# A four-layer transformer kernel on one core: products of a block of ones in TensorE's waits at twelve layer norms and two RMS norms

## What is computed

```
def layer_norm(x, g, b):
    mu = jnp.mean(xf, axis=-1, keepdims=True)
    var = jnp.mean(jnp.square(xf - mu), axis=-1, keepdims=True)
    y = (xf - mu) * lax.rsqrt(var + LN_EPS) * g + b
...
    for i in range(DEPTH_2):
        y = swa_sink_attention / rglru_block / mla_attention (x, ...)
        x = layer_norm(ALPHA * x + y, ln_g[i, 0], ln_b[i, 0])
        x = layer_norm(ALPHA * x + memory_cross_attention(x, ...), ln_g[i, 1], ln_b[i, 1])
        x = layer_norm(ALPHA * x + conv_glu_ffn(x, ...), ln_g[i, 2], ln_b[i, 2])
```

## Time and profile before

| | us |
|---|---|
| median of three runs | 2805.81 |
| lowest and highest run | 2800.55 and 2807.04 |
| span of the profiled execution, first to last instruction | 2794.0 |
| median less span | 11.8 |
| TensorE matmuls busy | 2636.5 |
| TensorE weight loads busy (beside matmuls) | 2501.8 |
| GpSimd busy | 1819.7 |
| ScalarE busy | 1467.7 |
| VectorE busy | 1126.3 |
| mean granted TensorE clock, share of full | 0.963 |

### The profile page before, as it was taken

One profiled execution on the slowest core, in us unless ns is written; L12 is line 12 of the kernel. 1 busy time (PEld: TensorE's weight loads), 2 busy tenths in 40 slices (PEclk: granted clock), 3 DMA queues, 4 the chain that ended last, 5 costly groups with the idle time before them and its releaser, 6 DMA issues.

```text
span 2794.0 us, 52649 instructions
## 1 busy us (share of the span) xinstructions
PE 2636.5 (94%) x19840; PEld 2501.8 (90%) x19840; DVE 1126.3 (40%) x2642; ACT 1467.7 (53%) x2586; POOL 1819.7 (65%) x770
## 2 busy tenths in 40 slices
PE   7998889999999999989999998999999999989998
PEld 5897779999997799988899988899978999988998
DVE  5227634122155521135443365433443433553334
ACT  5336734445445554444555576555645555555655
POOL 0446647878875778863578865488645688535886
PEclk7999999999999999999999999999999999989998
DMA  6324424555553555542345543355423455323554
GB/s 228 125 102 153 146 95 166 180 178 184 183 167 126 180 168 183 179 142 81 121 151 181 185 138 128 107 189 180 157 92 121 144 181 183 127 76 121 173 180 136
DMA packets 115637, 421.75 MB, mean 151 GB/s; under 512 B 12832, under 2 KB 14112, under 8 KB 114976
## 3 DMA queue, kind: packets, MB, share of 16 engines
q1 hardware_dynamic: 115200, 417.00, 45.2%
q10 hardware_dynamic: 288, 2.62, 0.2%
HBM read 418.52 MB, written 1.05 MB: 150 GB/s over the span
## 4 chain that ended last, share of the span: by engine, by line
PE 58%; issue 18%; POOL 15%; DVE 5%; ACT 2%; DMA 1%; POOLq 0%; SPq 0%; DVEq 0%; ACTq 0%
POOL ring_low L2444 15%; PE bank L610 10%; PE bank L611 10%; PE bank L616 10%; PE bank L601 7%; PE bank L602 7%; PE bank L603 7%; PE bank L916 2%; PE bank L885 2%; PE bank L766 1%; DMA ring<-in_units 1%; PE bank L705 1%; PE bank L934 1%; PE bank L706 1%; PE bank L899 1%
## 5 line engine op out<-in xcount | busy, mean ns | idle before, releaser
L2444 POOL TENSOR_TENSOR ring_low<-ring,ring_high 128x1024 fp32r<-128x1024 f32 x766 | 1819.5, 2405 | 954.5 <-ACT ring_high L1243 744.0
L610 PE MATMUL bank<-high,ring_high 128*128 128x256 f32 (+1 forms) x3372 | 857.1, 290 | 3.2 <-ACT ring_high L1243 1.8
L611 PE MATMUL bank<-low,ring_high 128*128 128x256 f32 (+1 forms) x3372 | 849.5, 288 | 0.0
L610 PEld LDWEIGHTS bank<-high,ring_high 128*128 128x128 f32 x3372 | 647.0, 192 | 10.5 <-ACT ring_high L1243 3.5
L611 PEld LDWEIGHTS bank<-low,ring_high 128*128 128x128 f32 x3372 | 647.2, 192 | 6.5
L1475 ACT ACTIVATE ring_high<-ring 128x1024 fp32r<-128x1024 f32 x448 | 468.3, 1054 | 90.8 <-DMA ring<-in_units 90.8
L616 PE MATMUL bank<-high,ring_low 128*128 128x256 f32 (+1 forms) x3372 | 491.3, 288 | 0.3 <-POOL ring_low L2444 0.3
L616 PEld LDWEIGHTS bank<-high,ring_low 128*128 128x128 f32 x3372 | 444.9, 192 | 6.1 <-POOL ring_low L2444 0.5
L1243 ACT ACTIVATE ring_high<-ring 128x1024 fp32r<-128x1024 f32 x337 | 351.4, 1054 | 101.1 <-DMA ring<-in_units 99.7
L601 PE MATMUL bank<-hid_high,ring_high 128*128 128x256 f32 x1232 | 349.5, 284 | 9.8 <-DVE hid_low L2091 7.4
L602 PE MATMUL bank<-hid_low,ring_high 128*128 128x256 f32 x1232 | 348.6, 283 | 0.0
(11 more groups left out here) (226 smaller groups left out, 3468.3 us busy)
## 6 DMA issues: line engine op xcount, KB each, us to landing
ring<-in_units SPq DMA_DIRECT2D x785, 512.0 KB, 3.4
xt<-in_x SPq DMA_DIRECT2D x2, 1024.0 KB, 8.4
nbias<-in_bias ACTq DMA_DIRECT2D x1, 1536.0 KB, 7.2
vt<-in_mem ACTq DMA_DIRECT2D x1, 1024.0 KB, 7.1
out_x<-xt SPq DMA_DIRECT2D x8, 128.0 KB, 1.7
consts<-in_consts SPq DMA_DIRECT2D x1, 832.0 KB, 9.9
cols<-in_cols SPq DMA_DIRECT2D x1, 639.0 KB, 6.3
consts<-in_consts SPq DMA_DIRECT2D x1, 512.0 KB, 7.5
```

Source lines behind the costliest of these rows:

```text
L610: first = pe.matmul(out, w[0], x[0], start=start, stop=False)
L611: pe.matmul(out, w[0], x[1], start=False, stop=False)
L2444: pool.tensor_tensor(whole(ring_low, u), whole(ring, u), whole(ring_high, u).bitcast(fp32), ALU.subtract).then_inc(unit_ready, 1)
```

## The change

A new helper `idle_products(n)` claims bank 4 and writes n fp32 products of `ones` by `ones`, 128 x 128, into it. Nobody reads them. `spread` now issues one product before it waits for `mean`, `between` products before it waits for `scale` (6 in token norms, 3 behind a feed-forward), and 7 after the last transposes, except in the last norm. `stats_summed` issues 20 products behind its statistics in `f0` and 18 in `f10`. Nothing else is changed; the RMS norms named `n10` and `n11`, and those in the mixer of layer 2, get none.

```
+                def idle_products(n):
+
+                    claim(4)
+                    for _ in range(n):
+                        pe.matmul(banks[4][:, 0:P], ones[:, :], ones[:, :], start=True, stop=True)
+
-                def spread(st):
+                def spread(st, between):
 
                     for name, b, at in (("mean", 7, 0), ("scale", 6, 6)):
                         claim(b)
+                        idle_products(1 if name == "mean" else between)
                         pe.wait_ge(*when(st, name))
...
                         reader[b] = (st, name + "_read")
+                    if st != f"ln{LAYERS2 - 1}2":
+                        idle_products(7)
...
-                    spread(st)
+                    spread(st, 3)
...
-                        spread(st)
+                        spread(st, 6)
...
-                def stats_summed(st, n=T, b=7, behind=KD - 1, total=None):
+                def stats_summed(st, n=T, b=7, behind=KD - 1, total=None, idle=0):
...
                         reader[b] = (st, "statsread")
+                        if idle:
+                            idle_products(idle)
...
-                        after=stats_summed("f0", n=2 * T))
+                        after=stats_summed("f0", n=2 * T, idle=20))
...
-                        after=stats_summed("f10"))
+                        after=stats_summed("f10", idle=18))
```

## The result

The changed kernel takes 2782.18 us, the median of seven runs (2779.17 to 2789.36), against 2796.6 us of the kernel before in the same comparison (seven runs, 2790.99 to 2807.04): ratio 0.9946, with a 95% interval from 0.9928 to 0.9965. That is about 15 us less, 10 to 20. I forecast 18 less.

What follows compares the result with a forecast made beforehand. TensorE, busy 94% of the span, was taken as the bound. Token norms 12, norms behind feed-forwards 2, `f0` and `f10` 4.3, `ln32` -0.6 make 18 us less: 2805.8 - 18 = 2788 us, range 2782 to 2794.

Steps and rivals of the forecast that it cites:

- Price of a product: Each fp32 128-column product on TensorE: two passes of 0.11 us, 0.22 us at 2.4 GHz, 0.43 at 1.2 GHz.
- `f0` and `f10`: Matmuls behind these two statistics: all time at the low clock counts, 0.44 x 9.7 = 4.3 us gained.
- Token norms, gain if the clock holds: Eight token norms: 14.6 us in their 72 matmuls plus 1.6 from faster scale transposes, 16.2 together.
- I take one of three norms to fall nevertheless: Token norms: the clock falls in a third, which gain 0.5 us instead of 2.0, so eight give 12 us.
- These waits are counted from TensorE's own matmuls and from slots that it sets free, so they move with it: Waits for weights and `hid_low`: an earlier TensorE shifts them along, so they do not swallow the gain.
- rival 4: Behind the starts, an early TensorE waits for weights or VectorE: gain only 6 us, 2800; chance 0.05.
- Norms behind a feed-forward: Three norms: scale 0.5 us late, most low-clock loss recovered; 0.7 us each, between -0.2 and 1.5, 2 us in all.
- `ln32`: Last norm, nothing follows: three cold products end 0.6 us behind the time of its scale transposes, -0.6 us.
- Rival 1: Most token norms fall despite the products, from one-column matmuls and waits: 10 us gained, 2796; chance 0.12.
- 2: The clock holds everywhere, behind the feed-forwards too: 26 us gained, 2780; chance 0.10.
- 5: The clock falls and returns as before, with the products hidden: within 3 us, 2806; chance 0.03.
- slower rival: Products of constants into an unread bank don't hold the clock, running at 0.43 us: 18 us more, 2824; chance 0.04.

Runs made afterwards that it cites:

- one-column run: The changed kernel with the same 187 products, each with 1 moving column instead of 128: 2803.18 us.

## Why the prediction was right, and where it was wrong

The sign, the range and the size held: 18 us forecast, 15 measured with an interval of 10 to 20. The mechanism held too, but that the sum came out this near is in part luck: about 4 us too little was counted for the token norms, and 8.7 us that came back at the feed-forwards (in the profiled pair) were not counted at all.

- **Price of a product**: 0.22 us forecast, 0.224 measured, from transposes of the same width and type as the nearest row. That they would fit, with what margin, and that too many cost time, held: nothing waited for a product in the changed kernel's token norms, and with twelve everything did.
- **`f0` and `f10`**: 4.3 us forecast, 2.7 + 1.9 = 4.6 measured, none of it given back.
- **Token norms, gain if the clock holds**: 1.6 + 14.6 = 16.2 us forecast, 2.3 + 13.8 = 16.1 measured. The rule behind it, VectorE's pace of 1.12 us against 1.08, held to 0.1 us in each norm.
- **"I take one of three norms to fall nevertheless" is the first wrong step.** The clock fell at none, in any execution with the full numbers. I discounted 4 us for a fear; six products and seven, with one ahead of the mean, were enough at every token norm.
- **"These waits are counted from TensorE's own matmuls and from slots that it sets free, so they move with it" is the second, and the larger.** It was my argument against rival 4. True for the weight ring: the way from the 72nd matmul behind a layer's first norm to its second norm took 59.28 us in all four layers before, and 59.28 or 59.29 after. False at the four feed-forwards of the second block: ScalarE's chain counts from the norm, not from TensorE, and had 0.20 to 0.96 us of slack in the kernel before. 1.4 us went back at each, 5.7 in all, and 1.5 more at each where the longer wait let the clock fall (two there, three when run again). The row that could have told me was ScalarE's timeline at a feed-forward's start, which I had not read: I read who released TensorE (`hid_low`), and not what would release it next once TensorE was earlier. So rival 4, which I gave 0.05, is true in part, and the growth of the waits for `hid_low` (7.4 to 12.8 us) is the sign that I had named for it.
- **Norms behind a feed-forward**: 2 us forecast, 1.2 in the profiled pair (3.2 less 2.0), 2.2 by means over eleven executions. The late scale (0.66, 0.66 and 0.33 us, against 0.5) and the return of the clock ahead of the matmuls came as drawn; the first matmul was late by 0.64, 0.64 and 0.70.
- **`ln32`**: -0.6 forecast, -0.6 measured.
- The transposes' median came out at 0.32 us and not near 0.27 (0.42 before), since those behind a feed-forward still run at 1.2 GHz and a first transpose of a pair behind products takes longer.

- **Transposes and the clock**: I read the earlier trace rows as if transposes seemed to hold the clock. By the trace TensorE was busy for the whole 3.40 us of that window, and besides the transposes of line 899 it did two more transposes and four matmuls 512 columns wide. So the row doesn't show what transposes alone would do.

Rival 1 (the clock falls at most norms), 2 (it holds behind the feed-forwards too) and 5 are out by the windows. The slower rival's mechanism is real, as the one-column run shows, but constants of 128 columns hold the clock.

## What to carry to other kernels

Where a short wait on TensorE makes the matmuls behind it run at half speed, products that nobody reads can hold the clock, if their sum ends just ahead of what the wait is for: work their price out from a row of the same width and type, and read the granted clock behind them, since TensorE's busy time was the same here with one-column products, which held nothing. And before counting a saving, look at each engine whose work starts from the same event as the one that is sped up, and how much slack it has; here less than a microsecond of ScalarE's slack decided over some 9 us, and moving a table load of 1.28 us into an idle gap got it back.

## What else the runs showed

The granted clock differed between executions in the same attention (the first layer of the second block, where the score matmuls contract over 64 rows), without any edit there. The same times in two runs, the changed kernel again and the run with the table load early:

```profile
1296.80:1313.80 17.00, 17.00 (x83) 0.50 0.00 1
...
1296.80:1313.80 17.00, 13.71 (x117) 1.00 0.00 1
```

83 matmuls against 117 in 17 us. The two windows don't hold quite the same work; followed matmul by matmul, the same 80 took 16.5 us in the first run and 10.2 in the second. TensorE was busy throughout at the low clock, and the clock still didn't come back for 17 us. From the 72nd matmul behind `f10` to the copy of `ln00` it took 336.8 to 337.8 us in eight executions, 338.6 and 340.6 in two, and 344.6 to 345.6 in the three with 17 us at the low clock. The start, up to the statistics of `f0`, took 408.2 to 416.1 us. These two are the largest parts of the scatter between executions, and bigger than most single effects above; why the clock stays low for 17 us in one execution and not in another is open, and products in that attention were not tried. In the same way the way from the 72nd matmul behind `ln22` to the copy of `ln30` took 87.0 us in executions without a fall of the clock there, 87.2 with 3.4 us at the low clock, 90.4 with 10.2 and 93.4 with 17.1.

The Trainium skill, "TensorE: Matmul & The Clock Gate", Part 4 (PE-mode transpose), has it that transposes don't count as busy in the same way. No run here separates transposes from products. The sum that I had worked out with more norms falling (16 us) lies as near to the measured 15 as mine, but its condition isn't borne out, since the clock fell at none.
